# One wait split in three, and block-diagonal matrices written block by block, in the head-pair stage of a decoder layer

## The reference, cut to what matters

```python
def _wkv_step(S, inp):
    r, w, k, v, kk, kka = inp
    sa = jnp.einsum('bhij,bhj->bhi', S, -kk)
    S = S * w[:, :, None, :] + sa[..., None] * kka[:, :, None, :] + v[..., None] * k[:, :, None, :]
    y = jnp.einsum('bhij,bhj->bhi', S, r)
    return S, y
```

## Time and profile before

| | us |
|---|---|
| median of 3 runs (lowest, highest) | 4613.98 (4611.28, 4614.55) |
| profiled execution, its own time | 4623.73 |
| span of the profile, first to last instruction | 4622.2 |
| PE busy over the span | 4106.0 (89%) |
| DVE busy | 3160.1 (68%) |
| ACT busy | 1245.7 (27%) |
| POOL busy | 1545.8 (33%) |

### The profile page before, as it was taken

The page is one execution under the profiler, slowest core; times in us unless marked ns, Lnnn a source line. Parts: engine busy times, 40 slices in busy tenths (PEclk is TensorE's granted clock), DMA queues, the critical chain, the costliest instruction groups (busy, mean ns, idle before and its releaser), DMA issues. The chain is left out here.

```text
span 4622.2 us, 72314 instructions
## 1 busy us (share of the span) xinstructions
PE 4106.0 (89%) x29289; PEld 3860.4 (84%) x29289; DVE 3160.1 (68%) x4314; ACT 1245.7 (27%) x1563; POOL 1545.8 (33%) x793
## 2 busy tenths in 40 slices
PE   5996889889889866996999999999997999999997
PEld 4896777777778755995999999999997999999996
DVE  2563453553553544334997888889877999999997
ACT  1343221221221211113223332332322232232223
POOL 0332213212222211003346444444442444444441
PEclk7998888888888866997999999999998999999998
DMA  8221212212212111312234999999998999999984
GB/s 351 79 85 59 75 64 75 81 64 79 79 61 86 68 53 70 150 64 77 83 112 160 357 374 373 375 375 381 375 386 314 372 372 372 364 364 373 374 339 188
DMA packets 214281, 982.50 MB, mean 213 GB/s; under 512 B 21952, under 2 KB 101952, under 8 KB 106560
## 3 DMA queue, kind: packets, MB, share of 16 engines
q1 hardware_dynamic: 92256, 524.19, 29.8%
q0 software_dynamic: 57984, 409.37, 22.6%
q10 hardware_dynamic: 63840, 46.15, 3.0%
HBM read 917.54 MB, written 62.09 MB: 212 GB/s over the span
## 5 line engine op out<-in xcount | busy, mean ns | idle before, releaser
L93 PE MATMUL PS<-first_HH,tail_WH 128*128 128x352 f32 (+1 forms) x3072 | 976.7, 318 | 86.1 <-DVE tail_WL L2011 41.7
L95 PE MATMUL PS<-first_HH,tail_WL 128*128 128x352 f32 (+1 forms) x3072 | 961.4, 313 | 0.0
L94 PE MATMUL PS<-first_HL,tail_WH 128*128 128x352 f32 (+1 forms) x3072 | 958.9, 312 | 0.0
L93 PE MATMUL PS<-dn_BH,tail_WH 128*128 128x352 f32 x2048 | 669.9, 327 | 54.0 <-DVE tail_WL L2164 32.0
L2153 POOL DMA_INDIRECT dn_VR<-in_v_rows,tail_EI x192 | 469.6, 2446 | 593.6 <-DVEq L2199 554.4
L93 PEld LDWEIGHTS PS<-first_HH,tail_WH 128*128 128x128 f32 x3072 | 583.9, 190 | 97.6 <-DVE tail_WL L2011 52.7
L95 PE MATMUL PS<-dn_BH,tail_WL 128*128 128x352 f32 x2048 | 661.6, 323 | 0.0
L94 PE MATMUL PS<-dn_BL,tail_WH 128*128 128x352 f32 x2048 | 659.3, 322 | 0.0
L1937 POOL DMA_INDIRECT up_UR<-in_u_rows,tail_EI x192 | 438.6, 2284 | 497.0 <-DVEq L2031 475.9
L94 PEld LDWEIGHTS PS<-first_HL,tail_WH 128*128 128x128 f32 x3072 | 586.3, 191 | 0.5
L95 PEld LDWEIGHTS PS<-first_HH,tail_WL 128*128 128x128 f32 x3072 | 583.1, 190 | 0.0
(11 more groups left out here) (391 smaller groups left out, 7657.4 us busy)
## 6 DMA issues: line engine op xcount, KB each, us to landing
tail_WR<-in_peer_u SPq DMA_DIRECT2D x128, 1024.0 KB, 9.1
tail_WR<-in_peer_v SPq DMA_DIRECT2D x128, 1024.0 KB, 6.7
mix_RING<-in_w_ada SPq DMA_DIRECT2D x88, 1024.0 KB, 4.8
mix_RING<-in_w_in SPq DMA_DIRECT2D x38, 1024.0 KB, 4.8
tmp_z<-up_ZB ACTq DMA_DIRECT2D x128, 176.0 KB, 8.1
tmp_gd<-up_STG ACTq DMA_DIRECT2D x22, 1024.0 KB, 20.5
dn_GG<-tmp_gd SPq DMA_DIRECT2D x16, 1408.0 KB, 9.3
dn_ZI<-tmp_z SPq DMA_DIRECT2D x128, 176.0 KB, 5.0
```

What stands on the lines that cost most here:

```text
L93: nc.tensor.matmul(out, r32(wh), r32(xh), start=first, stop=False)
L94: nc.tensor.matmul(out, r32(wh), r32(xl), start=False, stop=False)
L95: return nc.tensor.matmul(out, r32(wl), r32(xh), start=False, stop=last)
```

## The change

The wait for `rows_used` is gone, and with it the semaphore. `evacuate` takes a flag `behind`; with it each copy that overwrites a buffer waits for that buffer: the first copy into `PP` for `pp_used` (DVE signals it behind the third mix of rows), the sigmoid into `WD` for `wd_used` (behind the last reader of `WD`), the one into `AG` for `ag_used`. `GN` is written and read by ACT alone.

The chunk matrices are formed from their diagonal blocks alone: two copies of 64 partitions for `K0`, two sums of 64 partitions for `GS` straight from PSUM and `DG`; the rest of both buffers is cleared once, at the start of the stage. `gk_read` is signalled behind all four, and `gk_ready` right behind it.

```diff
-        def evacuate(act, i, lo=0, hi=6):
+        def evacuate(act, i, lo=0, hi=6, behind=False):
...
                 act.wait_ge(proj_done, 6 * i + (which + 1))
+                if behind and which in (0, 3, 4):
+                    act.wait_ge({0: pp_used, 3: wd_used, 4: ag_used}[which], i)
...
                 if ahead:
-                    act.wait_ge(rows_used, i + 1)
-                    evacuate(act, i + 1)
+                    evacuate(act, i + 1, behind=True)
...
                 if which == 1:
                     dve.sem_inc(act_rows, 1)
+            dve.sem_inc(pp_used, 1)
...
             dve.drain().then_inc(ss_ready, 1)
+            dve.sem_inc(wd_used, 1)
...
             V.tensor_tensor(DT[:, body], NR[:, body], AG[:, body], ALU.mult)
-            dve.drain()
+            dve.drain().then_inc(ag_used, 1)
...
-            dve.drain().then_inc(rows_used, 1)
-            dve.sem_inc(prep_ready, 1)
+            dve.drain().then_inc(prep_ready, 1)
...
-            bd = bcast(bcast(BD[:], 1, 4), 1, 2)
             by_chunk = lambda ap: ap.rearrange("p (x c) t -> p x c t", x=2)
             prod = PS[:, 0:4, :].rearrange("p c (x k t) -> p k x c t", x=2, k=2)
-            V.tensor_tensor(by_chunk(GS[:]), prod[:, 0], bd, ALU.mult)
+            blocks = [slice(64 * h, 64 * h + 64) for h in range(2)]
             if step == 0:
                 dve.wait_ge(so_free, i + 1)
-            V.tensor_tensor(by_chunk(K0[:]), prod[:, 1], bd, ALU.mult)
+            for at in blocks:
+                V.tensor_copy(by_chunk(K0[at])[:, :, :, at], prod[at, 1][:, :, :, at])
+            dve.wait_ge(dg_ready, u + 1)
+            for at in blocks:
+                V.tensor_tensor(by_chunk(GS[at])[:, :, :, at], prod[at, 0][:, :, :, at], by_chunk(DG[at])[:, :, :, at],
+                                ALU.add)
             dve.drain().then_inc(gk_read, 1)
-            dve.wait_ge(dg_ready, u + 1)
-            V.tensor_tensor(GS[:], GS[:], DG, ALU.add)
-            dve.drain().then_inc(gk_ready, 1)
+            dve.sem_inc(gk_ready, 1)
             dve.sem_inc(gk_free, 1)
...
-            for buf in (PP, WD, SLT, SI, SB, CHN, SUMS):
+            for buf in (PP, WD, SLT, SI, SB, CHN, SUMS, GS, K0):
```

More of the change, by code:

```diff
@@ L748, in phase_rwkv @@
     ada_in, ada_used, mr_ready, turned, mod_read = (m.sem(x) for x in "ada_in ada_used mr_ready turned mod_read".split())
-    (cleared, slot_used, proj_done, proj_ev, gk_free, banks_idle, act_rows, rows_used, sq_ready, ss_done, ss_ready,
+    (cleared, slot_used, proj_done, proj_ev, gk_free, banks_idle, act_rows, sq_ready, ss_done, ss_ready,
      nr_ready, rk_ready, bo_done, rows_in, g2_free, prep_ready, tr_done, tr_ready, mm_prod, mm_ready, lt_ready,
@@ L752, in phase_rwkv @@
      r2_ready, gk_done, gk_read, gk_ready, s_done, s_ready, yy_done, yt_ready, mean_done, yc_ready, ysq_ready, var_done,
-     sd_ready, post_done, mix_free, so_ready, so_free, sp_ready, sp_free) = (m.sem(x) for x in (
-        "cleared slot_used proj_done proj_ev gk_free banks_idle act_rows rows_used sq_ready ss_done ss_ready "
+     sd_ready, post_done, mix_free, so_ready, so_free, sp_ready, sp_free, pp_used, wd_used,
+     ag_used) = (m.sem(x) for x in (
+        "cleared slot_used proj_done proj_ev gk_free banks_idle act_rows sq_ready ss_done ss_ready "
         "nr_ready rk_ready bo_done rows_in g2_free prep_ready tr_done tr_ready mm_prod mm_ready lt_ready "
@@ L757, in phase_rwkv @@
         "r2_ready gk_done gk_read gk_ready s_done s_ready yy_done yt_ready mean_done yc_ready ysq_ready var_done "
-        "sd_ready post_done mix_free so_ready so_free sp_ready sp_free").split())
+        "sd_ready post_done mix_free so_ready so_free sp_ready sp_free pp_used wd_used ag_used").split())
     PC0, PC1 = 1 + SEQ, W1
```

## The result

The changed kernel takes 4573.76 us (median of four, 4566.72 to 4577.1) against 4612.63 for the kernel before beside it: ratio 0.9907, interval [0.9889, 0.9924], so a gain of 35 to 51 us. The forecast was 4560, a gain of 54; the time lies within its range of 4546 to 4580, but the gain falls short of the middle value. The profiled execution took 4577.1 us with a span of 4575.5; before, the span was 4622.2. So the two profiles lie 46.6 us apart.

What follows compares the result with a forecast made beforehand. Between projections and first transposes PE, DVE and ACT were taken to work in turn, that chain setting the pair's time. 51.0 + 5.6 - 6.6 + 3.8 = 53.8 us, taken from the median 4613.98: 4560, range 4546 to 4580.

Steps and rivals of the forecast that it cites:

- The gap: From second `head_sum` to first transposes, seven pairs: 105.9 us falls to 7.85 each, gain 51.0, bounds 47.8 to 53.4.
- Rivals 1 and 4: Narrow projections at the lower clock, 4588, chance 0.08; the split wait not doing what it says, 4617, chance 0.02.
- The later `gk_read`: At 16 step boundaries, four instructions strictly one behind another: +0.41 us each, 6.6 lost, bounds 2.1 to 15.2.
- The samples' wait: Behind the third step, PE's wait for `gk_ready` shrinks: gain 3.8 us, bounds 0 and 9.5.
- the three short waits: Three of PE's five waits behind the third step, attributed to POOL working in SBUF: 1.9 us, to vanish.
- The clock of the first step: First 3.77 us of each first step, at 0.55 before: gain 0.8 a pair, 5.6 us, bounds -12.6 to +11.9.
- the row I named as the sign: Clock row of the first 3.8 us of a step, which was to read 1.00.
- Rivals 2 and 3: First step at the upper clock throughout, 4541, chance 0.07; falling to the lower and staying, 4727, chance 0.03.
- what makes it later is paid in full: At all 16 step boundaries PE's products waited for `gk_read`, 23.2 us; any delay counts at its own length.

Runs made afterwards that it cites:

- the eight fillers: Changed kernel plus eight small matmuls, results unread, on PE ahead of the first step's transposes in each pair: 4600.85 us, ratio 0.9964.
- the split alone: Changed kernel with the old chunk-matrix instructions put back, only the copies' separate waits kept: 4565.1 us, ratio 0.9897.
- the blocks alone: Changed kernel with the copies' one wait for `rows_used` put back, chunk matrices still by diagonal blocks: 4623.99 us, ratio 1.0012.
- the later signal: Separate copy waits with old chunk matrices, plus a product of 384 elements done twice ahead of `gk_read`: 4586.83 us, ratio 0.9933.
- the filled boundary: Changed kernel plus three small matmuls, results unread, on PE between transposes and products at each step boundary: 4601.93 us, ratio 0.9965.
- the padded kernel: Changed kernel plus sixteen small matmuls once at the start of the stage, none in the pairs: 4613.97 us, ratio 0.9991.

## Why the prediction was right, and where it was not

- **The gap: right.** Forecast 51.0, measured 50.3; the gap 7.85 forecast, 7.93 to 8.02 measured. The projections at 1.2 us, ACT's chain and the 2.80 of the Exp came as worked out. Rivals 1 and 4 are out.
- **The later `gk_read`: right in its direct price.** Forecast 6.6, measured 16 x 0.44 = 7.0; the middle value, one strictly behind another, was the one.
- **The samples' wait: right.** Forecast a gain of 3.8, with two waits of about 2.9 left; measured 9.5 - 6.0 = 3.5, two left of 3.0 at most. The reason given for the three short waits, a sum slowed while POOL works in SBUF, is borne out: six of the 24 sums took 3.6 to 5.2 us before, none of the 48 after took over 0.8. But the split removes these waits as well, though six of its sums still take 4.8 to 5.1, so on top of the split the blocks are worth 7.6 - 6.0 = 1.6, not 3.8, and no time shows it.
- **The clock of the first step: too large.** I took 5.6 us because the idle stretch of rows 6 stood at 1.00. Measured is 1.9 over the eight pairs, and the row I named as the sign, the first 3.8 us, reads 0.55 instead of 1.00: the idle stretch shows a full clock and the work behind it pays. With the eight fillers the same step gained a further 8.5, so the clock was to be had, but not by shortening the idle time from 3.83 + 2.80 to 2.80. Rivals 2 and 3 are out: it neither stayed up nor stayed down.
- **Missing: the clock behind the boundary.** The failed step is "what makes it later is paid in full": it was paid with more on top. Step 2 lost 10.4 us, of which 8 x 0.44 = 3.5 are the wait; the other 6.9 go with the clock. Shown by the split alone (loss gone), the blocks alone (loss there), the later signal (loss there without blocks), the filled boundary (loss gone with the late signal). Over all profiles no step 2 is longer than 36.7 us where the boundary idles 1.45 us or less (56 pairs in seven kernels), and from two to six of eight are over 37.5 where it idles 1.79 or more. Why one pair is hit and the next is spared stays open.
- **Step 3.** Against its own 3.5 of longer wait it gained 3.5 at the samples and 3.9 elsewhere; the sixth pair alone, 36.25 us, is 5.3 shorter than before. In the padded kernel, which does the same work, the second pair is at 36.24 and the sixth at 41.66, so I take it for where the clock happened to fall, not for an effect of the change.

Together: 50.3 - 1.4 + 1.9 - 7.0 + 3.5 - 6.9 + 3.9 + 0.9 = 45.2 for the stage, against 53.8 forecast; the difference is 3.7 in the first step's clock, 6.9 in the second's and 1.4 between the `head_sum`s, less the 3.9 and 0.9 gained elsewhere, and 1.4 in smaller terms. Head and tail differ by several microseconds from profile to profile where nothing was changed (481.7 to 488.2 for all heads, 2794.6 to 2807.6 for the tails of the kernels with 140 packets), so single profiles and medians can disagree by about as much.

That the time lies within the range is in part luck. The range's 20 us on the slow side rest above all on the bound for the first step's clock, 18.2 us below the value taken, while most of what was missing lay in the second step. The fast side of the range is also wrong in itself: with the bounds of the four terms taken as independent, as it says, the gain reaches 64 us and not 68.

What was left lies in the same clock: with PE's two idle times filled, the changed kernel falls to 4550.77 and the split alone to 4545.49; by the ratios (0.9907 to 0.9856, 0.9897 to 0.9838) that is 24 and 27 us.

## What to carry to other kernels

A wait that an edit lengthens on TensorE has two prices, its own length and the granted clock of the work behind it; read the granted clock of the microseconds after each idle time, not of the idle time itself. The second is not paid in every round: here it was paid in two to six pairs of eight. Where such an idle time cannot be removed, a few matmuls that nobody reads can be worth more than the wait. And when an edit adds instructions to an engine, compare the instruction queue's packets and the waits for issue of loops that the edit does not touch.

## What was not expected of the hardware

- 0.44 us more idle time at a boundary (1.45 to 1.89) moved the fall of the granted clock from 7.4 to 4.0 us into the step and made the stretch at 1.2 GHz 13.6 us long instead of 6.8, in four pairs of eight. At the same 1.89 us the other runs have two, five and six long second steps, at 2.09 six, and at 1.45 or less none.
- Sixteen or eighteen matmuls more in PE's program cost 33 to 40 us in a later loop that they do not touch, with 203 packets of instructions instead of 140; thirty-four cost nothing there.
